# Two products for three: both parts of the input against the high weights, in the gate and up projections of a two-block layer stack

## What is computed

```
def swiglu_ffn(u, w_gate, w_up, w_down):            # block 1, two in each layer, width 2816
    return (jax.nn.silu(u @ w_gate) * (u @ w_up)) @ w_down
...
u = jax.nn.relu(rmsnorm(x, norm_ffn) @ w_ff1)       # block 2, one in each layer, width 4096
return x + (u * u) @ w_ff2
...
a_cs = jnp.cumsum(a, axis=-1)                       # block 1's state-space mixer, 16 heads
seg = jnp.exp(jnp.where(causal, a_cs[..., :, None] - a_cs[..., None, :], NEG_INF))
```

## Time and profile before

| | |
|---|---|
| median of 3 runs | 2806.37 us |
| the profiled execution | 2803.35 us, span 2801.7 us |
| TensorE busy | 2654.6 us (95%), 19771 products |
| VectorE, ScalarE, GpSimd busy | 1779.5 (64%), 1181.2 (42%), 1000.6 us (36%) |
| mean granted clock of TensorE | 0.977 |
| read from memory | 475.87 MB, 171 GB/s |

### The profile page before, as it was taken

How to read it: one execution, slowest core, us unless ns; L and a number is a source line. 1 busy time by engine, 2 the same in 40 slices (tenths; PEclk the granted TensorE clock), 3 DMA queues, 4 the chain that set the end, 5 groups by cost and what they waited for, 6 DMA issues and landing times.

```text
span 2801.7 us, 51457 instructions
## 1 busy us (share of the span) xinstructions
PE 2654.6 (95%) x19771; PEld 2486.5 (89%) x19776; DVE 1779.5 (64%) x2796; ACT 1181.2 (42%) x1979; POOL 1000.6 (36%) x588
## 2 busy tenths in 40 slices
PE   4999999899999999999999998998988999988999
PEld 3999999778889989989987888998977999977899
DVE  6764897466376586559955754765644676554576
ACT  2444445145244454444442543444442444442444
POOL 2434876200033323378650001433640244540244
PEclk9999999799999999999998999999999999999999
DMA  8775753233376576767431335763433555433454
GB/s 322 265 270 189 252 179 124 73 98 113 121 263 234 185 260 235 240 218 233 144 127 63 98 113 204 263 210 120 130 96 113 157 184 162 133 102 105 150 188 135
DMA packets 131491, 481.35 MB, mean 172 GB/s; under 512 B 14848, under 2 KB 14848, under 8 KB 130560
## 3 DMA queue, kind: packets, MB, share of 16 engines
q1 hardware_dynamic: 107280, 389.12, 42.5%
q0 software_dynamic: 23040, 83.90, 8.2%
q10 hardware_dynamic: 1008, 6.06, 0.6%
HBM read 475.87 MB, written 3.15 MB: 171 GB/s over the span
## 4 chain that ended last, share of the span: by engine, by line
PE 84%; DVE 9%; ACT 3%; POOL 1%; DVEq 1%; issue 1%; DMA 0%; SPq 0%; ACTq 0%
PE ps L432 20%; PE ps L434 19%; PE ps L433 19%; PE ps L672 5%; PE ps L2192 2%; PE ps L975 2%; PE ps L526 2%; PE ps L442 1%; PE ps L443 1%; PE ps L441 1%; PE ps L2158 1%; PE ps L474 1%; POOL ring_parts L1857 1%; PE ps L895 1%; DVE pt L1933 1%
## 5 line engine op out<-in xcount | busy, mean ns | idle before, releaser
L433 PE MATMUL ps<-u_parts,high 128*128 128x256 f32 x3712 | 1056.0, 284 | 0.0
L433 PEld LDWEIGHTS ps<-u_parts,high 128*128 128x128 f32 x3712 | 711.4, 192 | 2.0
L1021 ACT ACTIVATE high<-ring 128x1024 fp32r<-128x1024 f32 x437 | 460.6, 1056 | 436.8 <-PE ps L434 331.8
L432 PE MATMUL ps<-ac_parts,high 128*128 128x256 f32 x1920 | 549.6, 286 | 24.0 <-DVE u_parts L1398 13.7
L434 PE MATMUL ps<-ac_parts,ring_parts 128*128 128x256 f32 x1920 | 545.9, 284 | 0.0
L1862 POOL TENSOR_TENSOR ring_parts<-ring,high 128x1024 fp32r<-128x1024 f32 x88 | 225.1, 2558 | 474.8 <-ACT high L1021 474.8
L432 PEld LDWEIGHTS ps<-ac_parts,high 128*128 128x128 f32 x1920 | 366.7, 191 | 30.0 <-issue 21.6
L432 PE MATMUL ps<-h_parts,high 128*128 128x256 f32 x1296 | 376.4, 290 | 6.6 <-POOL ring_parts L1857 4.4
L1857 POOL TENSOR_TENSOR ring_parts<-ring,high 128x1024 fp32r<-128x1024 f32 x138 | 331.7, 2412 | 138.3 <-ACT high L1021 136.7
L434 PE MATMUL ps<-h_parts,ring_parts 128*128 128x256 f32 x1296 | 369.2, 285 | 0.0
L434 PEld LDWEIGHTS ps<-ac_parts,ring_parts 128*128 128x128 f32 x1920 | 365.3, 190 | 0.0
(11 more groups left out here) (430 smaller groups left out, 5047.6 us busy)
## 6 DMA issues: line engine op xcount, KB each, us to landing
ring<-stream_dram SPq DMA_DIRECT2D x736, 512.0 KB, 3.6
xc<-ada_dram POOLq DMA_DIRECT2D x84, 512.0 KB, 6.1
z<-ada_dram POOLq DMA_DIRECT2D x36, 512.0 KB, 7.0
qr<-ada_dram POOLq DMA_DIRECT2D x36, 512.0 KB, 6.1
h_aside<-ac ACTq DMA_DIRECT2D x2, 1024.0 KB, 3.8
eb<-ada_dram POOLq DMA_DIRECT2D x4, 512.0 KB, 5.4
h<-h_aside ACTq DMA_DIRECT2D x2, 1024.0 KB, 5.9
conb<-con_dram ACTq DMA_DIRECT2D x1, 1088.0 KB, 6.3
```

The source lines that it names most:

```text
L432: mm(out, hi, xh, start=start, stop=False, **kw)
L433: mm(out, hi, xl, start=False, stop=False, **kw)
L1021: act(high_of(m, i), chunk_of(m, i), ACT.Copy).then_inc(made, 1)
```

## The change

`product2` takes the place of `product3` in the gate and up projections of block 1 and in the first projection of block 2. One product of 512 columns takes the high weights against both input parts (the tiles `ac` and `u` now lie behind one another in one buffer, seen as `both_ffn`), and one of 256 columns adds the low weights times the high input to the second half. The sum is in two halves of 256 columns; VectorE adds them with a `tensor_reduce`. In block 1 gate and up have a bank each, 4 + 2(f % 2) + c, and silu and the hidden product now work on the summed values in memory; `sums` and low(i+3) stand ahead of the hidden product in VectorE's queue. Bank 7 has two uses, so `column_sums` waits for the hidden value of the step before, and TensorE waits for `keep_columns` (semaphore `kept`) ahead of the second chunk of the steps j = 0 and f = 19. In block 2 VectorE adds the halves and does relu and square in one operation; ScalarE's relu goes. The decays are split by ScalarE and VectorE into two rounded parts and spread by two float32r products.

```
+def product2(mm, out, m, i, k, both, xh, start, stop, **kw):
+    a, b = k * P, k * P + P
+    mm(out.rearrange("p (b t) -> p b t", b=2), high_of(m, i)[:, a:b], both, start=start, stop=False, **kw)
+    return mm(out[:, S:2 * S], low_of(m, i)[:, a:b], xh, start=False, stop=stop, **kw)
...
-            def up(i, f, fk):
+            def up(i, f, fk, kept=None):
                 for c in range(2):
                     t.wait_ge(sem["lo"], at("lo", 2 * NF * q + 2 * fk + c + 1))
+                    if c == 1 and kept is not None:
+                        t.wait_ge(ada.kept, kept)
                     for k in range(ND):
-                        last = product3(mm, ps[:, 4 + f % 3, c * S:(c + 1) * S], m, i + c, k, m.uhi_ffn[:, k], m.ulo[:, k],
-                                        start=k == 0, stop=k == ND - 1)
+                        last = product2(mm, ps[:, 4 + 2 * (f % 2) + c, :], m, i + c, k, m.both_ffn[:, k], m.uhi_ffn[:, k],
+                                        start=k == 0, stop=k == ND - 1, skip_group_check=True)
...
-                    up(cb + 2 + 3 * j, 1 + j, 6 * it + 1 + j)
+                    up(cb + 2 + 3 * j, 1 + j, 6 * it + 1 + j, ada.summed_group(l, q, it) if j == 0 else None)
                     if j == 5:
+                        t.wait_ge(sem["hid"], at("hid", q * NF + 6 * it + 6))
                         column_sums(t, mm, m, ada, ada.summed_group(l, q, it))
...
         def decay(h):
-            mm(ps[:, unit(j), 0:S], m.con[0:16, CON["ident"] + h:CON["ident"] + h + 1].to_broadcast([16, P]),
-               m.decay, start=True, stop=True).then_inc(sem["bc"], 1)
+            row = m.ident_r[:, h:h + 1].to_broadcast([16, P])
+            mm(ps[:, unit(j), 0:S], row, m.decay_hi, start=True, stop=False)
+            mm(ps[:, unit(j), 0:S], row, m.decay_lo, start=False, stop=True).then_inc(sem["bc"], 1)
...
-            def silu(i, f, rounds=0):
-                a.wait_ge(done, done_at(i, rounds))
-                act(m.silu[:, f % 3], ps[:, 4 + f % 3, 0:S], ACT.Silu).then_inc(sem["silu"], 1)
+            def silu(f, fk):
+                a.wait_ge(sem["sums"], at("sums", q * NF + fk + 1))
+                act(m.silu[:, f % 3], m.silu[:, f % 3], ACT.Silu).then_inc(sem["silu"], 1)
...
-    nc.vector.tensor_copy(m.raw[:, 16:24], m.ps[:, 7, 0:8])
+    nc.vector.tensor_copy(m.raw[:, 16:24], m.ps[:, 7, 0:8]).then_inc(ada.kept, 1)
...
+            def sums(i, f, rounds=0):
+                v.wait_ge(done, done_at(i, rounds))
+                b = 4 + 2 * (f % 2)
+                for c, dst in ((1, m.hid), (0, m.silu)):
+                    last = nc.vector.tensor_reduce(dst[:, f % 3], ps[:, b + c, :].rearrange("p (h t) -> p t h", h=2), AX, ALU.add)
+                last.then_inc(sem["sums"], 1)
...
-                tt(m.hid[:, f % 3], ps[:, b, S:2 * S], m.silu[:, f % 3], ALU.mult).then_inc(sem["hid"], 1)
+                tt(m.hid[:, f % 3], m.hid[:, f % 3], m.silu[:, f % 3], ALU.mult).then_inc(sem["hid"], 1)
...
+                    sums(i, f, it * 2)
+                    low(i + 3, HIGHS * q + 3 * fk + 4)
                     hidden(f, fk)
-                    low(i + 3, HIGHS * q + 3 * fk + 4)
                     hidden_low(f, fk)
...
+        v.wait_ge(sem["acsc"], at("acsc", 1))
+        tt(m.decay_lo, ps[0:16, bank(j + 1), S:2 * S], m.decay_hi, ALU.subtract)
...
-        def hidden(f, fk):
-            v.wait_ge(sem["relu"], at("relu", fk + 1))
-            tt(m.hid[:, f % 3], m.silu[:, f % 3], m.silu[:, f % 3], ALU.mult).then_inc(sem["hid"], 1)
+        def hidden(i, f, rounds=0):
+            v.wait_ge(done, done_at(i, rounds))
+            t, b = m.silu[:, f % 3], 4 + f % 3
+            nc.vector.tensor_reduce(t, ps[:, b, :].rearrange("p (h t) -> p t h", h=2), AX, ALU.add)
+            v.drain()
+            stt(m.hid[:, f % 3], t, 0.0, t, ALU.max, ALU.mult).then_inc(sem["hid"], 1)
```

More of the change, by code:

```diff
@@ L208, in __init__ @@
         self.used, self.summed, self.columns = sem("ada_used"), sem("ada_summed"), sem("ada_columns")
-        self.rows, self.mixed = sem("ada_rows"), sem("ada_mixed")
+        self.rows, self.mixed, self.kept = sem("ada_rows"), sem("ada_mixed"), sem("ada_kept")
     def group(self, l, stage, it=0):
@@ L244 @@
     layer_done=1, par=16, umod=24, uhi=24, ulo=24, hi=6 * NF + MIX1, lo=4 * NF, lo_m=MIX1 - FRONT, lo_g=2 * NF + FRONT,
-    aside=16, back=16, whole=24, based=3, pairs=6, silu=2 * NF, hid=2 * NF, hidhi=2 * NF, hidlo=2 * NF, resid=24, mu=4, cent=32,
+    aside=16, back=16, whole=24, based=3, pairs=6, sums=2 * NF, silu=2 * NF, hid=2 * NF, hidhi=2 * NF, hidlo=2 * NF, resid=24, mu=4, cent=32,
     sq=40, var=5, sd=5, sg=8, glu=8, copied=23, aconv=8, xconv=16, xsilu=16, kpe=2, rotp=12, rope=12,
@@ L281, in memory @@
     m.high = sb("high", HIGH * 1024, F32R)
[L283 to L286, removed]
+    acts, acts_parts = typed_twice("acts", 4 * ND * S)
+    part = lambda t, n: t[:, n * ND * S:(n + 1) * ND * S]
+    h, hparts = part(acts, 0), part(acts_parts, 0)
+    m.h, m.uhi = tiles(h, ND), tiles(hparts, ND)
+    u, ulo = part(acts, 1), part(acts_parts, 1)
+    m.u, m.ulo = tiles(u, ND), tiles(ulo, ND)
     eb = sb("eb", 2048)
-    cmp_, cmp_parts = typed_twice("cmp", 2048)
+    cmp_, cmp_parts = part(acts, 3), part(acts_parts, 3)
     m.par2 = sb("par2", DEPTH * PAR2["all"])
@@ L294, in memory @@
     ap_ = sb("ap", ND * (S + TAPS_A - 1))
-    ac, acr = typed_twice("ac", ND * S)
+    ac, acr = part(acts, 2), part(acts_parts, 2)
+    m.both_ffn = acts_parts[:, ND * S:3 * ND * S].rearrange("p (b n t) -> p n b t", b=2, n=ND)
     xp = sb("xp", NXB * (S + TAPS_B - 1))
@@ L756, in layer @@
             else:
-                t.wait_ge(sem["acsc"], at("acsc", 1))
+                t.wait_ge(sem["xdt"], at("xdt", 1))
             t.wait_ge(sem["xsilu"], at("xsilu", 8))
@@ L1057, in step @@
             def step(i, f, fk, rounds=0):
-                silu(i, f, rounds)
+                silu(f, fk)
                 later_high(i + 3, rounds)
@@ L1064, in ffn @@
             later_high(cb + 3)
-            silu(cb + 1, 0)
+            silu(0, 0)
             later_high(cb + 4)
@@ L1074, in ffn @@
                 step(cb + 3 * f, f, f)
-            silu(cb + 63, 21)
+            silu(21, 21)
             hidden_high(21, 21)
@@ L1199, in layer @@
         act(m.nacs, ps[:, bank(j), 0:32], ACT.Copy, scale=-1.0)
-        act(m.decay, ps[0:16, bank(j), S:2 * S], ACT.Copy).then_inc(sem["acsc"], 1)
+        act(m.ident_r, m.con[0:16, CON["ident"]:CON["ident"] + 16], ACT.Copy)
+        act(m.decay_hi, ps[0:16, bank(j), S:2 * S], ACT.Copy).then_inc(sem["acsc"], 1)
         j += 5
@@ L1447, in hidden_low @@
                     .then_inc(sem["hidlo"], 1)
+            sums(cb + 1, 0)
             low(cb + 3, HIGHS * q + 4)
@@ L1466, in ffn @@
             for f in range(19, 21):
+                sums(cb + 3 * f, f)
+                low(cb + 3 * f + 3, HIGHS * q + 3 * f + 4)
                 hidden(f, f)
-                low(cb + 3 * f + 3, HIGHS * q + 3 * f + 4)
                 hidden_low(f, f)
@@ L1471, in ffn @@
                     low(cb + 3 * f + 5, HIGHS * q + 3 * f + 6)
+            sums(cb + 63, 21)
             keep()
@@ L2630, in hidden_low, with step @@
                 .then_inc(sem["hidlo"], 1)
-        def step(f, fk):
-            hidden(f, fk)
+        def step(i, f, fk, rounds=0):
+            hidden(i, f, rounds)
             hidden_low(f, fk)
@@ L2636, in step @@
                 low(E_FFN + 2 * f + 3, 2 * fk + 4)
[L2638 removed]
+        step(E_FFN, 0, 0)
         with v.Fori(0, 3) as it:
             for q in range(9):
[L2641 removed]
+                step(E_FFN + 1 + 2 * q, 1 + q, 9 * it + 1 + q, 2 * it)
         for f in range(28, NF2):
[L2643 removed]
+            step(E_FFN + 2 * f - 1, f, f)
         for q in range(4):
```

32 lines of the change are left out of this document (13 added, 19 removed).

## The result

The kernel after takes 2991.4 us (median of 4 runs, 2991.2 to 2994.1) against 2806.35 us of the kernel before on the same chip: a ratio of 1.066 [1.064, 1.068], 185 us more. The profiled execution took 2991.23 us, 187.9 more than that of before. The forecast was 2951, the range 2892 to 3025.

A forecast was written before the change was run, and what follows sets the result against it. TensorE bounds the kernel now; after the change VectorE's sequence sets block 1's pace. Block 1 +160, block 2 -10, decays -5: +145 on 2803.35 gives 2948, plus 3.0 to the median, 2951 us; range 2892 to 3025.

The forecast's parts named there:

- The bound and the sign: Whole kernel: TensorE falls to VectorE's pace in block 1, stays the bound in block 2; slower, chance 0.89.
- The step with modulation: Block 1, steps with modulation rows: VectorE's cycle 11.1 us against 8.54 before, +2.56 us a step.
- (c): Block 1: the chain binds but the reductions are short, 0.42 us; +101, 2907 us, chance 0.17.
- (d): Block 1: the reductions take 1.0 us; +195, 3001 us, chance 0.14.
- Rival (a): Whole kernel: TensorE stays the bound everywhere, so the change is faster; 2763 us, chance 0.06.
- Where TensorE's waits would show: Block 1: TensorE idle some 160 to 190 us behind VectorE's low parts, plus 12 waits behind the kept-column copy.
- The wait on kept columns: Block 1, second chunk of j = 0 and f = 19: 12 waits; +2.3 us for the j = 5 step.
- rival (e): Block 1: waits let the clock fall, 2.7 us more behind each; +32 on the forecast, 2983 us, chance 0.08.
- The 512-column product: Gate and up groups: 512- and 256-column products for three of 256; gain 20 ns a group, 0.16 us a chunk.
- Block 2: First projection's steps: TensorE stays the bound, new step 5.53 us, 64 x 0.16 = -10 us.
- Decays: Decay products: at most -12 us, half taken, -6, and +1 for VectorE's wait on the copy and its subtraction.
- The sum: Whole kernel: +160 - 10 - 5 = +145 us on the profiled execution's 2803.35, forecast 2951 us.

The follow-up runs named there:

- both moves: Changed kernel with high(i+3) ahead of silu(f) in ScalarE's queue and keep_columns ahead of low(i+5) in VectorE's: 2818.4 us, 1.005 of the kernel before.
- three moves: Changed kernel with high(i+3) ahead of silu, keep_columns ahead of low(i+5), and one modulation row ahead of the hidden low part: 2799.4 us, 0.998 of the kernel before.

## Why the prediction came out as it did

**The bound and the sign: right.** VectorE's order sets the pace in block 1, TensorE in block 2. That the same reductions cost 12 us in the old order and the exchange of silu and high(i+3) gives back 120 shows that in block 1 it's the order.

**The step with modulation: right, by its own rows.** Forecast 11.1 us, measured 11.00; the wait ahead of low(i+3) 1.4, measured 1.43; reductions 1.35, measured 1.28; hidden low at 4.90 after T, measured 4.76 (150.14 - 145.38). The next reductions come as the last low part ends, as in the forecast's sequence. Rivals (c) and (d) fall with the reduction's 682 ns on average. Rival (a) fails at its own condition: reductions, silu and high cost VectorE 2.7 us a step. The order was free to choose, though: with both moves the stage is at 204 us. The forecast named the cause but gave no price of the other order.

**Where TensorE's waits would show: wrong in the name.** Forecast were 160 to 190 us behind VectorE's low parts. Measured over three kinds it is 109 us, too little even with the 0.16 us a wait that the list leaves out: 31.9 behind those low parts, 65.8 behind GpSimd's and 11.0 behind the hidden low part. The sequence had high(i+4) from 4.77 and GpSimd from 5.87, but wasn't followed to the down chunk that needs it. Counted from the start of the reductions, GpSimd's low part ends after 8.6 us, and TensorE needs 2.72 + 2 x 2.79 = 8.3 from the end of the up chunk, which in the steady steps lies 2.2 us before the reductions begin. Behind either engine TensorE is held to VectorE's cycle of 11.0 us, since GpSimd's low part follows, through ScalarE, from VectorE's hidden product. So the pace was right, with the wrong releaser for most of the waiting.

**The wait on kept columns: the step that was mis-sized.** Forecast +2.3 us for each step j = 5, 28 in all, and the clock as rival (e) at 0.08. Measured were waits of 4.4 us on average, 52.9 in all, and 77 us back when the copy moves up. The copy came where the forecast had it: it ends 9.6 us after the reductions began (129.24 - 119.66) against 9.75. What was mis-sized is the chunk behind it, 5.3 us where 2.7 stood: the three steps j = 5 of the first stage last 15.2, 14.1 and 14.8 us, where 12.5 was forecast. Rival (e) was no alternative to the forecast but a part of it: 2951 + 32 = 2983 is 8 us from the result. The forecast had the evidence, the clock of 0.67 in the earlier trace rows, and the waits, "about 5 us long". It put a low chance on a fall of the clock because "the steps are otherwise dense". The turns show the same: low parts behind the copy begin at 126.31, 194.20 and 260.97, so turns are 67.9 and 66.8 us where 65 to 67 stood, and stages are 246 where 232 to 240 stood.

**The 512-column product: about half the forecast gain.** A pair takes 0.349 us (the starts of L447 from 122.01 to 124.45, seven intervals) and 0.347 over the first stage of the kernel with three moves, against 3 x 0.119 = 0.357, so 8 to 10 ns a group are gained, not 20. The zero product's 99 ns for 256 further columns was too good a price: the 512-column product is followed after 0.23 us, not 0.218, and the 256-column one behind it after 0.115. Of the two sides that the forecast weighed, the rule in the Trainium skill, TensorE: Matmul & The Clock Gate, section "Back-to-back issue gap", gives for a product by itself what comes, as an estimate, to 325 ns a pair at the full clock and a gain of 2; the trace has 349 and 8, so neither its level nor the gain agrees. Its other line, N/1.2 ns at the low clock, gives 427 and 213, and there the trace agrees: 0.42 and 0.22.

**Block 2: right in the step of one stage, partly by luck.** In the first stage the step fell by 0.16 us as forecast, in the second by 0.09, from 5.60. Part of the 0.16 has nothing to do with `product2`: with the decays alone, three products in block 2, the step is 5.60 us in both stages. These traces show two paces of a stream of three products: 0.118 us from product to product throughout (first stage of the kernel before), or 0.119 to 0.120 in the first chunk and 0.113 to 0.114 in the down chunk (its second stage, and the kernel with the decays alone). What decides between them is open; the new places of the buffers can't be all of it, since the second stage of the kernel before has the faster one too. `product2` itself is worth the rest, 0.09 us a step, 6 us in all, where 10 were forecast. From 2150 us on, the six profiled executions with block 2's part are 6.8 to 8.6 us shorter than the one of the kernel before, the three others without it 1.8 shorter to 2.1 longer. The medians with and without it differ by 5 us, on two chips; against the kernel before beside each, by 2, which is within the intervals. Hidden low takes 2.15 us, close to the 2.42 of the earlier trace rows, and ends 0.3 us behind GpSimd's subtraction (2532.09 to 2534.49): the trace agrees again with the shared lock that the forecast took from the Trainium skill, SBUF: State Buffer.

**Decays: right in sign, small.** Forecast -6 of at most -12 for the products, and +1; measured -15 by the medians, -8.1 in the mixers of the profiled execution. The products explain 6.7, as forecast.

**The sum.** Forecast +145, measured +185. Of the 40 us between, the kept columns are 49 too few (28 forecast, 77 given back when the copy moves up), and all the rest 9 too many (117 forecast, 108 left by that run). By the experiments: some 170 for the two orders and 15 for what is left, of which the parts of block 2 and of the decays are -17; so block 1's part costs 32 us even in the better order, and 19 to 22 of these go when one modulation row is moved.

## What to carry to other kernels

When an operation moves from one engine's input to another's, read what stands behind it in the in-order queue: here silu's new cause held up an independent copy behind it, and two exchanged lines were worth 120 us, the added arithmetic 12. Follow each delayed producer to its consumer, also across the third engine. Price a new wait of a dense TensorE stream with the slow chunk behind it, not with its length alone, and test parts of a bundled change apart: the two small parts gained 17 us while the large one lost.

## What the runs showed of the hardware

- A wait of 4.33 us put TensorE at 1.2 GHz for a whole chunk (5.3 us where 2.8 is usual), and the clock fell behind all twelve waits of 4.3 to 4.5 us (0.50 to 0.76 over 6 us). Waits of 2.8 us did it in eight of twelve cases, and then for part of a chunk (0.72 over 6 us); in the kernel with the high part ahead of silu, whose waits are as long, it fell behind all twelve (0.50 to 0.76).
- A float32r product of 512 columns with its weight load is followed after 0.23 us and one of 256 after 0.115: two products and weight loads in place of three, for the same columns, bring 2 to 3%.
- A reduction of 512 PSUM values took 0.69 us with 256 results and 691 ns with 4: the number of results costs nothing here.
- A dense stream of 256-column float32r products ran at 0.118 us a product in one stage of block 2 and, in the down chunks of the other, at 0.113, in one execution of the kernel before and at a granted clock of 1.00 in both (2190 to 2360 and 2635 to 2795 us). A step was 5.67 us in the one and 5.60 in the other. What decides it is open.
